# Delta mixer: a level's two convolution pieces ahead of the turn on VectorE, and key norm sums in front of the solves

## What is computed

```python
def mixer_c(h, w_in, conv_w, A_log, dt_bias, norm_w, w_out):
    z = h @ w_in
    qkv = jax.nn.silu(causal_dwconv(z[..., :3 * W], conv_w))      # width-4 convolution over positions
    ...
    q = l2norm(qkv[..., :W].reshape(b, s, DN_HEADS, DN_HEAD_DIM)) * (DN_HEAD_DIM ** -0.5)
    k = l2norm(qkv[..., W:2 * W].reshape(b, s, DN_HEADS, DN_HEAD_DIM))
    o = gated_delta_rule_chunked(q, k, v, g, beta)
    ...

def gated_delta_rule_chunked(q, k, v, g, beta):                   # chunks of 64 positions, 8 heads
    A = jnp.where(strict, beta[..., :, None] * kk * decay, 0.0)
    sol = lax.linalg.triangular_solve(A + eye, rhs, left_side=True, lower=True, unit_diagonal=True)
    ...
```

## Time and profile before

| | |
|---|---|
| median of 3 runs | 2232.56 us (2231.41 to 2233.32) |
| profiled execution, its own time | 2233.46 us |
| span of its trace | 2231.7 us |
| TensorE matmuls busy | 2136.9 us, 96% |
| VectorE busy | 1161.1 us, 52% |
| ScalarE busy | 762.6 us, 34% |
| GpSimd busy | 202.7 us, 9% |
| pairs of heads (first to last of the levels) | about 1525 to 1780 us |

### The profile page before, as it was taken

The page is one execution under the profiler, slowest core; times in us unless marked ns, Lnnn a source line. Parts: engine busy times, 40 slices in busy tenths (PEclk is TensorE's granted clock), DMA queues, the critical chain, the costliest instruction groups (busy, mean ns, idle before and its releaser), DMA issues. The chain is left out here.

```text
span 2231.7 us, 33545 instructions
## 1 busy us (share of the span) xinstructions
PE 2136.9 (96%) x13572; PEld 1756.5 (79%) x13572; DVE 1161.1 (52%) x1450; ACT 762.6 (34%) x1045; POOL 202.7 (9%) x137
## 2 busy tenths in 40 slices
PE   6999999998888999999999999998999999999997
PEld 4888888775886888888888888877887778888886
DVE  5444443658647544444444443477667665444423
ACT  4322322345224323322323332254554453223221
POOL 2000011000421000001000001103212210000010
PEclk9999999999999999999999999999999999999999
DMA  4333332320012333332233333221111123333331
GB/s 157 94 94 99 111 103 64 109 76 1 3 41 69 92 99 99 94 117 92 75 104 94 94 113 103 76 85 40 39 40 48 50 65 95 94 98 100 113 92 49
DMA packets 48271, 182.95 MB, mean 82 GB/s; under 512 B 6320, under 2 KB 6576, under 8 KB 48048
## 3 DMA queue, kind: packets, MB, share of 16 engines
q1 hardware_dynamic: 48176, 181.58, 26.5%
HBM read 179.46 MB, written 2.10 MB: 81 GB/s over the span
## 5 line engine op out<-in xcount | busy, mean ns | idle before, releaser
L542 PE MATMUL banks<-H,WS 128*128 128x512 f32 x1840 | 735.3, 400 | 26.0 <-DVE WS L1564 16.6
L544 PE MATMUL banks<-H,WS 128*128 128x512 f32 x1840 | 722.0, 392 | 0.0
L543 PE MATMUL banks<-H,WS 128*128 128x512 f32 x1840 | 721.7, 392 | 0.0
L1091 ACT ACTIVATE WS<-RAW 128x1024 fp32r<-128x1024 f32 (+1 forms) x310 | 349.1, 1126 | 994.5 <-PE banks L544 993.1
L1564 DVE TENSOR_TENSOR WS<-RAW,WS 128x1024 fp32r<-128x1024 f32 (+1 forms) x310 | 408.7, 1319 | 217.6 <-ACT WS L1091 217.4
L542 PEld LDWEIGHTS banks<-H,WS 128*128 128x128 f32 x1840 | 347.9, 189 | 106.5 <-DVE WS L1564 14.1
L544 PEld LDWEIGHTS banks<-H,WS 128*128 128x128 f32 x1840 | 348.4, 189 | 73.9
L543 PEld LDWEIGHTS banks<-H,WS 128*128 128x128 f32 x1840 | 348.6, 189 | 71.1 <-issue 1.9
L544 PE MATMUL banks<-A,WS 128*128 128x512 f32 x704 | 274.1, 389 | 0.0
L543 PE MATMUL banks<-A,WS 128*128 128x512 f32 x704 | 274.1, 389 | 0.0
L542 PE MATMUL banks<-A,WS 128*128 128x512 f32 x704 | 274.1, 389 | 0.0
(11 more groups left out here) (337 smaller groups left out, 1802.3 us busy)
## 6 DMA issues: line engine op xcount, KB each, us to landing
RAW<-in_w_gate SPq DMA_DIRECT2D x88, 512.0 KB, 3.6
RAW<-in_w_up SPq DMA_DIRECT2D x88, 512.0 KB, 3.6
RAW<-in_w_down SPq DMA_DIRECT2D x64, 704.0 KB, 4.0
RAW<-in_c_in SPq DMA_DIRECT2D x32, 512.0 KB, 3.6
RAW<-in_ab_in SPq DMA_DIRECT2D x22, 512.0 KB, 3.7
RAW<-in_ab_out SPq DMA_DIRECT2D x8, 512.0 KB, 4.6
RAW<-in_c_out SPq DMA_DIRECT2D x8, 512.0 KB, 3.7
X<-in_x SPq DMA_DIRECT2D x4, 512.0 KB, 6.7
```

The source lines that it names most:

```text
L542: pe.matmul(bank[:, :], WS[:, 0, s, cols], src[0][:, r, :], start=first and j == 0, stop=False)
L543: pe.matmul(bank[:, :], WS[:, 0, s, cols], src[1][:, r, :], start=False, stop=False)
L544: mm = pe.matmul(bank[:, :], WS[:, 1, s, cols], src[0][:, r, :], start=False, stop=last and j == len(rows) - 1)
L1091: act.activation(WS[:, 0, c % SPLIT, 0:cols], RAW[:, c % RING, 0:cols], ACT.Copy).then_inc(hi_ready, 1)
```

## The change

On VectorE, in levels 0 to 3, the wait for `c_XX` and the turn go behind the level's second piece; `query_scaled` thereby stands ahead of the turn. The key norm arithmetic goes behind the first two pieces that follow the levels. On TensorE the key norm sums go from behind the first join product (with the slot and L987 behind them) to directly ahead of the solves.

```diff
@@ TensorE
                         mm.then_inc(c_u21_mm.sem, 1)
-                        if p < 3:
-                            key_norms(p + 1)
                         slot()
                         pe.wait_ge(*c_u21(p + 1))
                         pe.wait_ge(*c_xt32(2 * p + 2))
@@
                         mm.then_inc(c_xt64_mm.sem, 1)
                         slot()
 
+                        if p < 3:
+                            key_norms(p + 1)
                         pe.wait_ge(*c_xt64(p + 1))
@@ VectorE
                             if l == 1:
                                 query_decays()
                             piece()
+                            if l in (3, 4):
+                                query_scaled(l - 3)
+                            piece()
                             if l < 4:
                                 vec.wait_ge(*c_xx(5 * p + l + 1))
                                 turn_crossed()
-                            if l in (3, 4):
-                                query_scaled(l - 3)
-                            piece()
+                        piece()
+                        piece()
                         if p < 3:
                             key_norms(p + 1)
-                        piece()
-                        piece()
                         piece()
                         piece()
```

## The result

The changed kernel takes 2224.1 us (median of 6, 2222.88 to 2225.3) against 2232.97 us (6 runs, 2231.41 to 2236.26): a ratio of 0.9956, with a 95% interval of 0.9946 to 0.9967, so the gain of 0.4% is clear of the noise. Its profiled execution took 2225.3 us with a span of 2223.5 us, 8.2 us under the span of before.

What follows compares the result with a forecast made beforehand. TensorE, busy 96% of the span, was taken as the bound, so only its waits and clock count: 2233.46 less 3.9 us of waits and 4.5 us of clock gives 2225.1, say 2225.0 us; range 2220.5 to 2230.0.

Steps and rivals of the forecast that it cites:

- The sum: Whole kernel: from 2233.46 us, less 3.9 us of waits and 4.5 us of clock, to 2225.0 us.
- The two terms: TensorE's waits for L2087 shrink by 3.9 of 9.2 us; clock falls in the joins go, 4.5 us.
- Level 2 to 3: Pair 1: taps and L1976 no longer queue for GpSimd's mask; TensorE's 1.38 us wait goes.
- Level 3 to 4: Pair 1: L2079 and L1564 queue for GpSimd; wait 1.2 us instead of 0.76, level 4's product 0.94 us earlier.
- the signs named: TensorE's waits: 1.0 to 1.4 us ahead of level 4 (1.8 in pair 3), 5 to 6 us for L2087 in all.
- The rival without queueing: Levels: no piece queues for GpSimd, all 9.2 us of waits and 4.5 of clock go, 2219.8 us; chance 0.10.
- its opposite: VectorE's pieces queue behind all GpSimd holds of levels 2 and 3: 17.2 us of waits, 2241.5 us; chance 0.05.
- Pair 3: Last pair: level 2's wait of 0.67 us goes, but level 4's product starts later, 0.4 us lost.
- Key norms: TensorE, L978 to L997: clock falls go, 7.0 us at 1.00 in pairs 0 and 1, 4.5 us gained, no wait added.
- the clock rival: Waits shrink by 3.9 us, but clock falls stay or go to another thin stretch: 2229.5 us; chance 0.22.
- Part 3: VectorE's key norm sums, put behind two more pieces: cost 0, with some 6 us of cover.

Runs made afterwards that it cites:

- Experiments 3 and 4: Each against the changed kernel: 3 puts level 3's turn between the pieces, 2221.53 us; 4 puts both query scalings on level 4, 2220.89 us.
- Experiment 2: The changed kernel with the turns put back between the pieces, so only the key norm moves remain: 2228.78 us, ratio 0.9978.
- Turns alone: The changed kernel with the key norm moves undone on TensorE and VectorE: 2228.64 us (ratio 0.9965), run again 2225.45 us (0.9968).
- experiment 6: The changed kernel, but on level 0 VectorE makes c_IU (L2085) ahead of the piece that splits weights: 2222.39 us, ratio 0.9959.

## Why the prediction was right

*The sum.* 2225.0 us was forecast, with 3.9 us of waits and 4.5 us of clock. The profile shows 5.0 and 4.5 in the pairs and 0.4 more, less 1.7 us outside them. The two terms are right in kind and nearly in size; that the total fits to a few tenths is luck. The sum was 1.5 us short in the pairs, and falls outside the pairs, which it didn't have, took that back. The other profiled execution of the changed kernel, with the same waits and no fall in the pairs, took 2221.94 us.

*Level 2 to 3.* Right: the wait of 1.38 us went in pairs 0 to 2, and with it the queueing of the taps and of L1976.

*Level 3 to 4.* The mechanism was right, its size a little off: the signs named were waits of 1.0 to 1.4 us and 5 to 6 us in all, and 4.2 us were left. L2079 and L1564 met L1551 and the turn became late, as worked out; the wait is 0.95 us where I had 1.2, and 1.40 in pair 3 where I had 1.8. L2087 of level 3 started 1.08 us ahead of the product instead of 0.96, and the turn began 4.41 us behind it instead of 4.55: the two estimated lengths of 1.0 us for an L1551 and the distances added up 0.26 us too long in pair 1. Over the four pairs (0.15, 0.25, 0.25 and 0.4) that is the 1.1 us between 3.9 and 5.0. Experiments 3 and 4 show that it is the overlap with GpSimd's instructions: the same instructions in an order that misses GpSimd's work are at their shortest, and 0.6 us of work taken out of GpSimd's time brings 1.45 us. The prediction read from the earlier trace rows that the turns keep their length under GpSimd's work; in those rows no turn lies under it. The trace after bears it out: in pair 1 two turn instructions, L2023 from 1613.62 on, take their usual 0.89 us under the mask of 1613.74, which keeps its 1.29. The rival without queueing, 2219.8 us, and its opposite, 2241.5 us, both fall.

*Pair 3.* A loss of 0.4 us was forecast; its levels came out even (34.49 us from L946 to L997, 1741.52 to 1776.01, against 34.58, 1750.58 to 1785.16).

*Key norms.* In the profiled execution each number held: 7.0 us at 1.00 in pairs 0 and 1, nothing new waits. Experiment 2, with no wait changed, gained 5.0 us, and falls in the joins are gone in all eight kept traces with the new place, against five in nine joins with the old. But the sum took the falls of one trace as certain. Turns alone has executions at 2224 us, as fast as the changed kernel, and in its second comparison, whose trace has one fall in the joins where before has them in two pairs, it was only 1.1 us behind. Whether the turns themselves leave fewer falls to save, or chance does, no run shows: the other trace of turns alone has them in the same two pairs as before. What the clock rival feared, a fall in another stretch, happened at three places: one between levels 0 and 1, in exchange for one of the same 1.5 us, one ahead of the levels for 1.6 us, and one behind the pairs, where the stretch is 0.95 us longer.

*Part 3.* Right: VectorE's later key norm arithmetic made nothing wait.

## What to carry to other kernels

When VectorE and GpSimd are woven around a chain, sort VectorE's fillers by their operands: those with both inputs in SBUF go where GpSimd is idle, those with one in PSUM, and transposes, where it works; a filler put into GpSimd's time can cost about twice its length (1.30 us for a 0.69, 2.06 for a 1.22). Put the fillers into a stretch in which the chain's next input isn't there yet, and then look at which of GpSimd's instructions the earlier chain will start, as experiment 6 gave back two thirds of its gain to one of them. Small matmuls were cheaper here apart, between dense blocks, than in a row (no fall in 24 joins against five in nine), and a gain from the clock should be counted as a chance, over several executions, and not as one profile's sum.

## What the runs showed of the hardware

The clock is a matter of the execution, not of the program alone: the single times of the same turns-alone kernel lie anywhere from 2223.4 to 2231.5 us, and pair 1's stretch between the x products of levels 0 and 1 took 8.14 us at 0.79 in one execution of the changed kernel and 6.65 us at 1.00 in the other. That puts the price of one fall at 1.5 us here. TensorE's longest wait in the levels of the changed kernel is the 1.7 us ahead of L962, so the clock falls without a long stand, behind stretches of short waits and 64x64 products. The Trainium skill ("TensorE: Matmul & The Clock Gate", section "HAM oscillation — how this bites in real kernels") speaks of gaps longer than any in these levels; by that rule alone none of these falls should be, and here the trace differs.
